# High and low parts side by side, the first weight tile in two halves, and one product instead of several for three norms

## What is computed

```
# block 1
h = concat(meta_tokens, x)                      # 272 x 1024
a = rms_norm(h, norm_mix)
q_na, k_na, v_na, q_hg, z_f, z_b, i_hg, ... = split_cols(a @ w_in)   # q, k, v of attention;
                                                # z_f, z_b, i_hg of the gated recurrence
h = h + mix @ w_o;  h = h + relu(rms_norm(h, norm_mlp) @ w_up)**2 @ w_down
h = rms_norm(h, norm_final)[:, N_META:]
# block 2, layer "even", then layer "odd"; each begins with
h = rmsnorm(x, g) * (1 + scale) + shift         # scale, shift from silu(c) @ ada_w + ada_b
a, u, v, gate = split(h @ in_w)                 # even
gq, gk, gv, glr, sq, sk, sv, gate = split(h @ in_w)                  # odd; glr has 16 columns
log_a = log_sigmoid(glr @ gate_w + gate_b) / 16
```

## Time and profile before

| | |
|---|---|
| median of 3 runs | 843.55 us (843.42 to 844.45) |
| the profiled execution's own time | 844.48 us |
| its span, first to last instruction | 842.7 us |
| mean granted TensorE clock | 0.998 |
| TensorE matmul busy | 824.9 us, 98% of the span |
| VectorE, ScalarE, GpSimd busy | 630.7, 494.1, 111.2 us |
| DMA, mean over the span | 202 GB/s |
| DMA in the first and second fortieth of the span | 345 and 330 GB/s |

### The profile page before, as it was taken

One profiled execution on the slowest core, in us unless ns is written; L12 is line 12 of the kernel. 1 busy time (PEld: TensorE's weight loads), 2 busy tenths in 40 slices (PEclk: granted clock), 3 DMA queues, 4 the chain that ended last, 5 costly groups with the idle time before them and its releaser, 6 DMA issues.

```text
span 842.7 us, 16994 instructions
## 1 busy us (share of the span) xinstructions
PE 824.9 (98%) x6908; PEld 804.1 (95%) x6908; DVE 630.7 (75%) x1002; ACT 494.1 (59%) x878; POOL 111.2 (13%) x128
## 2 busy tenths in 40 slices
PE   5999999999999999999999999999999999999996
PEld 5998899998999999999999999999999999999995
DVE  4686568995896878787989798887888558555663
ACT  6454556663767646564666764464677366666652
POOL 0011255320120000000030530000202040000001
PEclk9999999999999999999999999999999999999999
DMA  9833344455666888989776677755655445555431
GB/s 345 330 102 103 117 153 126 127 163 196 214 190 194 311 336 283 366 283 388 253 251 185 220 221 228 248 190 189 198 166 184 127 126 174 203 152 152 148 99 51
DMA packets 46876, 170.40 MB, mean 202 GB/s; under 512 B 5200, under 2 KB 5456, under 8 KB 46544
## 3 DMA queue, kind: packets, MB, share of 16 engines
q1 hardware_dynamic: 46080, 165.31, 59.6%
q10 hardware_dynamic: 720, 4.01, 1.2%
HBM read 168.26 MB, written 1.05 MB: 201 GB/s over the span
## 4 chain that ended last, share of the span: by engine, by line
PE 93%; DVE 3%; ACT 1%; DMA 1%; issue 0%; POOL 0%; SPq 0%; DVEq 0%; POOLq 0%; ACTq 0%
PE bank L196 93%; DVE wl L235 1%; DMA raw<-in_ws 1%; DVE raw L223 1%; PE bank L199 0%; ACT wh L205 0%; DVE B1l L235 0%; ACT sq L202 0%; DVE vn L232 0%; POOL sq L235 0%; SPq L193 0%; DVE ga L223 0%; DVE gc L235 0%; ACT gb L202 0%; DVE pf L223 0%
## 5 line engine op out<-in xcount | busy, mean ns | idle before, releaser
L235 DVE TENSOR_TENSOR wl<-raw,wh 128x1024 fp32r<-128x1024 f32 x259 | 324.7, 1266 | 24.4 <-ACT wh L205 23.5
L205 ACT CAST wh<-raw 128x1024 fp32r<-128x1024 f32 x259 | 268.7, 1048 | 111.6 <-PE bank L196 60.8
L196 PE MATMUL bank<-XAh,wl 128*128 128x256 f32 (+1 forms) x896 | 255.2, 285 | 0.6 <-DVE wl L235 0.6
L196 PE MATMUL bank<-XAl,wh 128*128 128x256 f32 (+1 forms) x896 | 249.4, 278 | 0.0
L196 PE MATMUL bank<-XAh,wh 128*128 128x256 f32 (+1 forms) x896 | 249.3, 278 | 0.0
L196 PEld LDWEIGHTS bank<-XAh,wl 128*128 128x128 f32 x896 | 168.5, 188 | 2.8 <-issue 1.8
L196 PEld LDWEIGHTS bank<-XAl,wh 128*128 128x128 f32 x896 | 169.0, 189 | 0.0
L196 PEld LDWEIGHTS bank<-XAh,wh 128*128 128x128 f32 x896 | 168.8, 188 | 0.1
L196 PE MATMUL bank<-B1h,wl 128*128 128x256 f32 (+1 forms) x464 | 129.9, 280 | 0.0
L196 PE MATMUL bank<-B1h,wh 128*128 128x256 f32 (+1 forms) x464 | 128.7, 277 | 0.0
L196 PE MATMUL bank<-B1l,wh 128*128 128x256 f32 (+1 forms) x464 | 128.6, 277 | 0.0
(11 more groups left out here) (261 smaller groups left out, 1240.4 us busy)
## 6 DMA issues: line engine op xcount, KB each, us to landing
raw<-in_ws SPq DMA_DIRECT2D x307, 512.0 KB, 4.4
bias<-in_bias ACTq DMA_DIRECT2D x1, 1664.0 KB, 11.5
hK<-in_xk SPq DMA_DIRECT2D x4, 272.0 KB, 5.3
h<-in_xt ACTq DMA_DIRECT2D x1, 1088.0 KB, 6.3
out<-gc SPq DMA_DIRECT2D x4, 256.0 KB, 2.6
C<-in_cst SPq DMA_DIRECT2D x1, 512.0 KB, 7.9
crow<-in_crow ACTq DMA_DIRECT2D x1, 512.0 KB, 3.5
wT<-in_wt SPq DMA_DIRECT2D x1, 512.0 KB, 6.2
```

Source lines behind the costliest of these rows:

```text
L196: return self.real.matmul(*a, **k)
L205: return self.real.copy(*a, **k)
L235: return self.real.tensor_tensor(*a, **k)
```

## The change

Six edits, in the order of the program.

1. Unit 0's weights are loaded in two halves from ScalarE's queue, ahead of its table load; SyncE's queue begins with `P` and three pieces of `hK`, then `raw` 1. `wh` and `wl` of unit 0 are made in halves too, and TensorE waits for the second half at k = 2 only.
2. The norm's sum over `hK` is added up by VectorE (`sq_sum`) and is one product, placed after the third unit in place of four after the first. Unit 4's cast stands ahead of `rsK` on ScalarE.
3. The meta tokens of `XAh` get a second place (columns 272 to 304, `META2`) with 16 high and 16 low parts side by side. In the layer `i` they are 32 standing columns, two products in place of three; `iM`, `ATm` and `Hm` have 32 rows or columns, and the sum of both halves arises in the product that uses them.
4. The 16 columns of `glr` stand twice in the unit; VectorE overwrites the second copy's high part by the low part (`beside`). Two products for each block in place of three; the weights that follow (`gw`) stand twice as well.
5. GpSimd adds all eight squares at the sites `even` and `odd`, and TensorE makes one product after the second unit in place of three.
6. Buffers and semaphores to match.

```
         def sync_program(e):
             e.dma_start(P[:, :], par).then_inc(one["par"], 16)
-            for i in range(len(items)):
-                for n in {0: (0,), 1: (1, 2), 2: (3,)}.get(i, ()):
-                    e.dma_start(hK[:, 2 * n:2 * n + 2, :], xk[:, 2 * n:2 * n + 2, :]).then_inc(x_sem[n], 16)
-                if i == 3:
+            for n in range(3):
+                e.dma_start(hK[:, 2 * n:2 * n + 2, :], xk[:, 2 * n:2 * n + 2, :]).then_inc(x_sem[n], 16)
+            for i in range(1, len(items)):
+                if i == 2:
+                    e.dma_start(hK[:, 6:8, :], xk[:, 6:8, :]).then_inc(x_sem[3], 16)
+                if i == 4:
                     e.dma_start(C[:, :], cst).then_inc(one["cst"], 16)
...
             def mean_squares():
-                sums.clear()
-                side.take("sums", "mix")
-                e.wait_ge(one["cst"], 16)
-                for k in range(0, 8, 2):
-                    e.wait_ge(*at("sq_pair", k))
-                    e.matmul(bk("sums", "mix")[:, 0:272], cst_("ones"), sq[k // 2][:, :], start=k == 0,
-                             stop=k == 6).then_inc(*up("sums", ("mix", k)))
-                side.give(("sums", "mix"), ("rs", "mix"))
+                units.append(0)
+                if len(units) == 3:
+                    sums.clear()
+                    ps = side.take("sums", "mix")
+                    e.wait_ge(one["cst"], 16)
+                    e.wait_ge(*at("sq_sum", 6))
+                    e.matmul(ps[:, 0:272], cst_("ones"), sq[0][:, :], start=True, stop=True).then_inc(
+                        *up("sums", ("mix", 7)))
...
-            square_sums("even", ("down3", 7), ("rs", "even"))
+            square_sums("even", ("down3", 7), ("rs", "even"), todo=((), (7,)))
...
-            t_tiles("glr", "odd_in", 2048, 2176, F0, unnormed("odd"), lambda t: [("glr_norm", 0)], n1=258,
-                    width=128, ring_of=lambda t: side)
+            def low_rank(j, q, kn, tiles):
+
+                e.wait_ge(*at("beside", 0))
+                w2 = half(j)[0].rearrange("p (k n) -> p k n", n=128)
+                for k in range(8):
+                    for event in unnormed("odd")(k):
+                        e.wait_ge(*at(*event))
+                    for n in range(2):
+                        m = e.matmul(bk("glr", 0)[0:32, 0:258], w2[:, k, 0:32], F0[1 - n][:, k, 0:258],
+                                     start=k == 0 and n == 0, stop=k == 7 and n == 1)
+                m.then_inc(*up("mm", ("glr", 0), ("unit", j)))
...
+            e.dma_start(slot(0)[:, 0:512], ws[0][:, 0:512]).then_inc(one["w0"], 16)
+            e.dma_start(slot(0)[:, 512:1024], ws[0][:, 512:1024]).then_inc(raw_sem[0], 16)
             table(LN_SET)
...
+                if k == 0:
+                    e.wait_ge(one["w0"], 16)
+                    e.copy(half(0)[0][:, 0:512], slot(0)[:, 0:512]).then_inc(*up("first_high", 0))
...
+            feed_for(0)
+            rsqrt("mix", bk("sums", "mix")[:, 0:272], 272, ("sums", ("mix", 7)), rsK)
...
+                        e.tensor_copy(XAh[:, :, META2:META2 + 16], XAh[:, :, 0:16])
+                        e.wait_ge(*at("xa_low", ("mix", 7)))
+                        e.tensor_copy(XAh[:, :, META2 + 16:META2 + 32], XAl[:, :, 0:16]).then_inc(*up("meta2", 0))
```

More of the change, by code:

```diff
@@ L492, in build @@
         At = [sbt(pgl, f"At{i}", [128, 384]) for i in range(2)]
-        glr = sbt(pgl, "glr", [16, 256])
+        glr = sbt(pgl, "glr", [32, 256])
         A1 = sbt(pgl, "A1", [128, 4, 256])
@@ L512, in bk @@
             return banks[bank_of[key]] if c.known or key in bank_of else banks[0]
+        AT_ONCE = ("even", "odd")
         ALONE = ("k", "oo2", "zf", "a", "qk", "glr")
@@ L543, in build @@
         x_sem = [sem(f"l_x{i}") for i in range(4)]
-        one = {n: sem("l_" + n) for n in ("cst", "par", "crow", "bias", "negw", "h", "msk", "wT", "bS", "late", "out")}
+        one = {n: sem("l_" + n) for n in ("cst", "par", "crow", "bias", "negw", "h", "msk", "wT", "bS", "late", "w0", "out")}
         def landed(i):
@@ L683, in three_wide, with two_wide @@
                 return m
+            def two_wide(dst, a, b, first, last):
+                width = dst.shape[1]
+                for n in range(2):
+                    for c in range(0, width, 256):
+                        m = e.matmul(dst[:, c:c + 256], a, b[n][:, c:c + 256], start=first and n == 0 and c == 0,
+                                     stop=last and n == 1 and c + 256 == width)
+                return m
             def t_tiles(label, name, c0, c1, X, ready, freed, k0=0, nk=8, n0=0, n1=256, width=256, xk=0, t0=0,
@@ L702, in unit @@
                     for k, b, t in todo:
+                        if j == 0 and k == 2 and b == 0:
+                            e.wait_ge(*low_at(j))
                         for event in ready(xk + q + k):
@@ L783, in square_sum @@
             def square_sum(site, k, *freed):
-                if k == 5:
+                if k == 5 or site in AT_ONCE:
                     side.take("sums", site)
-                e.wait_ge(*(at("sq_add", (site, 5)) if k == 5 else at("sq", (site, k))))
+                e.wait_ge(*(at("sq_add", (site, k)) if k == 5 or site in AT_ONCE else at("sq", (site, k))))
                 e.wait_ge(one["cst"], 16)
-                e.matmul(bk("sums", site)[:, 0:256], cst_("ones"), sq_of(site, 0 if k == 5 else k)[:, 0:256],
-                         start=k == 5, stop=k == 7).then_inc(*up("sums", (site, k)))
+                e.matmul(bk("sums", site)[:, 0:256], cst_("ones"),
+                         sq_of(site, 0 if k == 5 or site in AT_ONCE else k)[:, 0:256], start=k == 5 or site in AT_ONCE,
+                         stop=k == 7).then_inc(*up("sums", (site, k)))
                 if k == 7:
@@ L1035, in tensor_program @@
                     lambda t: [("h_eo", (0, t))])
-            square_sums("odd", ("eo1", 7), ("rs", "odd"))
+            square_sums("odd", ("eo1", 7), ("rs", "odd"), todo=((), (7,)))
             t_tiles("eo1", "even_out", 0, 1024, (B1h, B1l), lambda k: [("yb0_high", k), ("yb0_low", k)],
@@ L1107, in tensor_program, with low_rank_done @@
             w.side += [odd_first(), gla()]
-            t_tiles("glr", "odd_in", 2048, 2176, F0, unnormed("odd"), lambda t: [("glr_norm", 0)], n1=258,
-                    width=128, ring_of=lambda t: side)
+            def low_rank(j, q, kn, tiles):
[4 more added lines that the diff above has]
+                        e.wait_ge(*at(*event))
+                    for n in range(2):
+                        m = e.matmul(bk("glr", 0)[0:32, 0:258], w2[:, k, 0:32], F0[1 - n][:, k, 0:258],
+                                     start=k == 0 and n == 0, stop=k == 7 and n == 1)
+                m.then_inc(*up("mm", ("glr", 0), ("unit", j)))
+            def low_rank_done(tiles):
+                side.give(("glr", 0), ("glr_norm", 0))
+            w.tiles("glr", "odd_in", 2048, 2176, lambda tiles: side.take("glr", 0), low_rank, low_rank_done, width=128)
             first("qk", "odd_in", F0, "odd")
@@ L1239, in square @@
                     return
-                if k < 6:
+                if k < 6 or site in AT_ONCE:
                     squares.give(n, ("sq_add", (site, k)))
@@ L1244, in square @@
                 if k == 7:
-                    squares.give(sq_at[site, 0], ("sums", (site, 5)))
+                    squares.give(sq_at[site, 0], ("sums", (site, 7 if site in AT_ONCE else 5)))
             def rsqrt(site, ps, N, after, rs=rsB):
@@ L1290, in scalar_program @@
                     e.wait_ge(*at("sq_pair", 0))
-            rsqrt("mix", bk("sums", "mix")[:, 0:272], 272, ("sums", ("mix", 6)), rsK)
+            feed_for(0)
+            rsqrt("mix", bk("sums", "mix")[:, 0:272], 272, ("sums", ("mix", 7)), rsK)
             e.dma_start(h[:, :, :], xt).then_inc(one["h"], 16)
@@ L1655, in odd_first @@
                         e.wait_ge(*at("glr_norm", 0))
-                        e.activation(glr[:, :], glr[:, :], ACT.Identity, bias=shc[0:16, 8:9]).then_inc(
+                        e.activation(glr[:, :], glr[:, :], ACT.Identity, bias=shc[0:32, 8:9]).then_inc(
                             *up("glr", 0))
@@ L1817, in feed_for @@
                         hi, lo = half(u)
-                        e.tensor_tensor(lo, slot(i), hi.bitcast(F32), ALU.subtract).then_inc(*up("low", u))
+                        c = slice(512 if u == 0 else 0, 1024)
+                        e.tensor_tensor(lo[:, c], slot(i)[:, c], hi[:, c].bitcast(F32), ALU.subtract).then_inc(
+                            *up("low", u))
+                        if it[5] == 128:
+                            hi, lo = (z.rearrange("p (k n) -> p k n", n=128)[:, :, 16:32] for z in (hi, lo))
+                            e.wait_ge(*now("low"))
+                            e.tensor_copy(hi, lo).then_inc(*up("beside", 0))
                         continue
@@ L1902, in vector_program @@
```

(5 more changed lines are left out.)

60 lines of the change are left out of this document (42 added, 18 removed).

## The result

| | before | changed |
|---|---|---|
| median of 4 runs beside each other | 843.48 us (842.85 to 844.45) | 837.21 us (836.83 to 838.09) |
| profiled execution, its span | 844.48, 842.7 us | 837.54, 835.5 us |
| TensorE busy, matmul instructions | 824.9 us, 6908 | 819.2 us, 6870 |
| first product, end of layer `k` | 8.91, 26.17 us | 7.53, 22.15 us |

The account below looks back on a forecast made before the run. TensorE, multiplying in 98% of the span, was taken as the bound. Gains of 5.2 (start and `k`), 1.8 (`i`), 0.4 (`glr`), 0.35 (`even`) and 0.86 (`odd`) made 8.6 us: 835.0 us predicted, range 833.2 to 837.3.

Parts of the forecast that it names:

- the case that had a chance of 0.60: Whole kernel: the time comes out as forecast, 833.9 to 836.0 us; chance 0.60.
- rival 2: Start: the clock rises at 13.8 us as before, not 4.9 us after the first product; 836.4 us; chance 0.12.
- Rival 3: Layer `k`: early units come late, `raw` 1 landing at 10.5 not 9.1; 836.4 us, at worst 837.4; chance 0.12.
- I let `hK` land at about 4.3, since it now shares the DMA engines with this half: Start: `hK` lands at about 4.3 us, so TensorE starts at 6.1, 2.8 us earlier.
- Half speed for 4.92 us after the first product: Start of layer `k`: the slow stretch again lasts 4.92 us, ending at 11.0 with 21 or 22 products done.
- Waits in `k`: Layer `k`: TensorE waits 0.1 us for unit 1 and 0.2 us at the one sum.
- Layer `i`: Products over the meta tokens: 16 of 48 go at 0.113 us each, a gain of 1.8 us.
- `glr`: Layer `glr`: eight of 24 products go, 0.96 us by count; waiting for `F0`'s low parts leaves a gain of 0.4.
- the chain from `eo1`'s last tile, not a product: Layer `glr`: what is late next after the eight products go; no size of its own.
- `even`: Norm sum at `even`: two sums fewer save 0.86 us, less a wait of 0.5; a gain of 0.35 us.
- the estimate of 4.1 us: Sum at `even`: two `wl` and two additions alternating take 4.1 us; a wait of 1.2, a loss of 0.3.
- `odd`: Norm sum at `odd`: two sums fewer, no wait, a gain of 0.86 us.

Follow-up runs that it names:

- warm start: The changed kernel with six products over zeros on TensorE ahead of the first real product; measured 837.11 us (ratio 0.9916).

## Why the prediction was right and wrong

The direction and the places of the gains were right. The size was not: 8.6 us were forecast and 6.3 measured. 837.21 lies at the far end of the range, which ended at 837.3, and outside the 833.9 to 836.0 of the case that had a chance of 0.60. The range reached so far for the sake of rivals 2 and 3, and neither of them happened, so that it held the result was luck. Two steps failed, worth about 1 us and 0.9 us.

- **The step that failed** first is "I let `hK` land at about 4.3, since it now shares the DMA engines with this half". The share was named and priced at 0.2 us; it cost 1.6 in the first profile (5.70 against 4.14) and 1.1 in the second. The ten profiles with the halves issued at about 0.74 on ScalarE's queue show `hK` at 5.3 to 5.8; the three with the halves behind it, by queue or by time, show 4.0 to 4.3, and the three with unit 0 whole behind it 4.1. That is shown. A price could have been had from the kernel before: there the first piece of `hK`, 272 KB, landed 1.35 us behind `P`, and an estimate at that rate for the 256 KB of the half that now lands between them is 1.3 us. The first product so came at 7.1 to 7.6 and not at 6.1. With the 0.3 us of forecast waits that did not come, `k` would end 0.7 to 1.2 us later than forecast for the same half-speed stretch; the two pairs of profiles show a gain of 4.0 (26.17 to 22.15) and 4.7 (25.75 to 21.02) at the end of `k`, where 5.2 was forecast. Moving the halves behind `hK` did not bring this back: the start was 0.9 us earlier and the median the same. The half was late in its turn, and runs differ by as much in their half-speed stretch; which of the two kept the median where it was is not shown.
- **The second step that failed** is the unwritten one that products keep their spacing when others are taken away. The prediction counted products and took 0.113 us for each in `gv` as given; there they stood 0.118 us apart, which is 0.93 us less gain. Its place in the sum is under `odd` below.
- **Half speed for 4.92 us after the first product**: 4.70 in the first profile by the prediction's own reading, so the term held, by luck. Over the profiles without a warm start the stretch is 3.3 to 5.3 us long. It always follows the first product, whenever that comes (rival 2 falls), and dummy products from 1.2 us on take it away altogether.
- **Waits in `k`**, 0.3 forecast: none, since TensorE came 1.4 us later than forecast and the feeds did not. Rival 3 falls too: `raw` 1 landed at 8.5 and not at 10.5, and unit 1's `wl` was ready at 11.53, 1.3 us before it was asked for. The warm start shows that it is the next limit.
- **Layer `i`** 1.8: measured 1.80, and without it the median was 2.6 higher, of which the trace explains 1.8. **`glr`** 0.4: 0.3, with the wait for `B0l` that was named; "the chain from `eo1`'s last tile, not a product" was right, and the edit is worth next to nothing.
- **`even`** 0.35: 0.17. The pair of additions took 3.45 us, just as the earlier trace rows had it, and the wait was 0.44 for 0.5. (433.35 and 3.45 are 436.8, not 436.9; it changes nothing.) The rows were the better guide than the estimate of 4.1 us, which went by the rule in the Trainium skill (SBUF — State Buffer, "SBUF: two separate sides"). What was left out is the price of a stop: from the last product before the sum to the sum are 0.72 us, 0.12 of spacing and 0.44 of idle time, so 0.16 more. One unit later there is no stop and 0.82 of the 0.86 comes.
- **`odd`** 0.86: right at its place, with no wait. But layer `gv` gave 0.8 to 0.9 back, so the edit at `odd` is worth about nothing. Why the spacing in `gv` changes from 0.113 to 0.118 us with the place of one product in the layer before it, some 23 us earlier, was not found and stays open.
- The extra 0.97 us before `eo0` was the chance of one run. The medians, 6.3 us apart, have less of it than the two first profiles.

## What to carry to other kernels

A load that is issued earlier on another queue is paid for by what is issued behind it on the first one: write the loads of both queues in one list by time of issue, look at which piece is waited for first, and count the bytes ahead of it before calling the overlap free. Where an added wait stands in a stream of products, try its product one unit later; it cost nothing at `even` here, and the stop cost more than its idle time. When a change removes a product, its gain is only sure once the spacing of the products in the layers behind it is read too, and one profile of each kernel does not tell a microsecond from the chance of a run.

## What the runs showed of the hardware

- The granted clock does not show the slow start. Two stretches of the changed kernel, before and after the spacing fell (us, busy, granted clock, DMA share, GB/s):

```profile
5.00:12.40 7.40, 4.87 (x21) 1.00 1.03 408
12.40:22.00 9.60, 9.60 (x78) 1.00 0.98 371
```

- Products of 256 columns start either 0.113 or 0.118 us apart for a whole layer, with nothing waited for and the granted clock at 1.00 in both. Before `eo0` the level changes with the run; in `gv` it follows the program.
- By the spacing (0.227 us for 272 columns, 1.2 GHz, then 0.124) the half-speed stretch ran for 3.3 to 5.3 us after TensorE's first product. Twelve instructions on zeros from 1.18 to 6.59 us ended it before the real work, and an idle time of 0.79 us after them did not bring it back. The Trainium skill (TensorE: Matmul & The Clock Gate, Part 1) has such a stretch as a time whose end varies from run to run; the runs agree that it varies, and their spread is 2 us.
- In all 16 traces the loads issued in the first 4.3 us landed in the order of their issue, over both queues. Two loads of 256 KB each issued from 2.67 us on took a median of 7.2 us to land; the same two issued from 0.74 on took 4.1.
